# Masked sample products of a hybrid HGRN/RWKV decoder step, cut into 32-column and 32-row tiles of four sequences

## What is computed

```python
def trunk(x, ...):
    h = rmsnorm(x, norm_mix); proj = h @ w_in
    o_hg, s_hg = hgrn2_mix(q, f_pre, i_in, g_in, lb, st_hg, ...)   # 4 heads, 128x128 state
    o_rw, s_rw = rwkv7_mix(proj[..., HG_COLS:], p_prev, st_rw, ...) # 8 heads, 64x64 state
    x = x + concat([o_hg, o_rw]) @ w_out
    x = x + moe_ffn(rmsnorm(x), ...)      # top 4 of 32 experts, 1024 -> 2x1024 -> 1024
    return rmsnorm(x, norm_final), s_hg, s_rw, h[:, -1]

# per sample sequence b (the prompt starts from a zero state):
o_inter = einsum('bhtk,bhkv->bhtv', qc * exp(G), S)                       # HGRN read
S = exp(G_last) * S + einsum('bhsk,bhsv->bhkv', kc * exp(G_last - G), ic) # HGRN update
S = S * w + sa (x) (kk * a) + v (x) k                                     # RWKV update, per token
```

## Time and profile before

| | |
|---|---|
| median of three runs | 1248.78 us (1248.23 to 1252.48) |
| span of the profiled execution | 1244.8 us |
| that execution's own time | not recorded apart; the median is 4.0 us over the span |
| TensorE busy | 1211.9 us (97%) |
| VectorE busy | 460.2 us (37%) |
| ScalarE busy | 255.2 us (21%) |
| moved by DMA | 436.11 MB, mean 350 GB/s |
| chain that ended last | TensorE 77%, DMA 18%, VectorE 3%, ScalarE 1% |

### The profile page before, as it was taken

The page is one execution under the profiler, slowest core; times in us unless marked ns, Lnnn a source line. Parts: engine busy times, 40 slices in busy tenths (PEclk is TensorE's granted clock), DMA queues, the critical chain, the costliest instruction groups (busy, mean ns, idle before and its releaser), DMA issues.

```text
span 1244.8 us, 18279 instructions
## 1 busy us (share of the span) xinstructions
PE 1211.9 (97%) x7854; PEld 584.8 (47%) x7854; DVE 460.2 (37%) x958; ACT 255.2 (21%) x619; POOL 39.6 (3%) x94
## 2 busy tenths in 40 slices
PE   8999999999999999999999999999999999999997
PEld 5777776745443434444444434434443444343332
DVE  2356986754312331333233223313322233132224
ACT  2113432521311102111111111121111111111113
POOL 7000010000100000000000000000000000000000
PEclk9999999999999999999999999999999999999999
DMA  9732102484999999999999999999999999999994
GB/s 281 175 93 78 53 27 71 125 339 191 377 426 427 427 427 427 432 434 427 432 430 429 433 429 432 428 432 430 431 429 432 431 427 434 429 430 431 426 424 173
DMA packets 45244, 436.11 MB, mean 350 GB/s; under 512 B 9045, under 2 KB 24472, under 8 KB 29162
## 3 DMA queue, kind: packets, MB, share of 16 engines
q1 hardware_dynamic: 44036, 431.35, 83.8%
q0 software_dynamic: 1040, 3.54, 0.9%
q10 hardware_dynamic: 86, 0.02, 0.0%
HBM read 430.01 MB, written 4.89 MB: 349 GB/s over the span
## 4 chain that ended last, share of the span: by engine, by line
PE 77%; DMA 18%; DVE 3%; ACT 1%; issue 0%; SPq 0%; DVEq 0%; ACTq 0%
PE bank L1457 28%; PE bank L1491 14%; PE bank L812 10%; DMA ring<-in_w_gate_up 9%; PE bank L1432 7%; DMA mix<-in_w_gate_up 6%; PE bank L1521 4%; PE bank L1247 3%; DMA mix<-in_w_down 2%; PE bank L1482 2%; PE bank L1005 1%; PE bank L1512 1%; DVE mix L2316 1%; PE bank L839 1%; DMA hx<-in_state_shift 0%
## 5 line engine op out<-in xcount | busy, mean ns | idle before, releaser
L1457 PE MATMUL bank<-ring,mix 128*64 128x512 f32 x1568 | 355.5, 596 | 11.7 <-DMA ring<-in_w_gate_up 10.9
L1457 PEld LDWEIGHTS bank<-ring,mix 128*64 128x64 f32 x1568 | 108.7, 137 | 227.1 <-issue 216.6
L1491 PE MATMUL bank<-ring,mix 128*64 128x512 f32 x736 | 167.8, 598 | 0.0
L2674 DVE TENSOR_TENSOR hTb<-bank,w2a 128x512 f32<-128x512 f32 x32 | 22.1, 691 | 373.7 <-PE bank L1482 373.7
L812 PE MATMUL bank<-hTb,ring 128*128 128x320 f32 (+1 forms) x480 | 139.1, 443 | 1.3 <-issue 1.3
L1991 ACT ACTIVATE mix<-bank,nf 128x256 f32<-128x256 f32 x64 | 26.9, 471 | 458.9 <-PE bank L1432 458.9
L1457 PE MATMUL bank<-mix 128*64 128x512 f32 x480 | 112.1, 599 | 1.3 <-DMA mix<-in_w_gate_up 1.2
L812 PEld LDWEIGHTS bank<-hTb,ring 128*128 128x128 f32 x480 | 89.5, 191 | 39.6 <-issue 3.7
L2726 DVE TENSOR_TENSOR mix<-mix,bank 128x512 f32<-128x512 f32 x70 | 48.2, 689 | 161.3 <-PE bank L1521 161.3
L1491 PEld LDWEIGHTS bank<-ring,mix 128*64 128x64 f32 x736 | 49.7, 136 | 87.4 <-issue 83.3
L1432 PE MATMUL bank<-mix,hx 128*128 128x256 f32 x256 | 70.0, 416 | 0.0
(11 more groups left out here) (422 smaller groups left out, 1099.9 us busy)
## 6 DMA issues: line engine op xcount, KB each, us to landing
ring<-in_w_gate_up SPq DMA_DIRECT2D x34, 4096.0 KB, 27.1
ring<-in_w_down SPq DMA_DIRECT2D x17, 4096.0 KB, 28.8
ring<-in_w_gate_up SPq DMA_DIRECT2D x30, 2048.0 KB, 14.5
mix<-in_w_gate_up SPq DMA_DIRECT2D x12, 4096.0 KB, 25.8
mix<-in_w_down SPq DMA_DIRECT2D x6, 4096.0 KB, 29.0
ring<-in_w_down SPq DMA_DIRECT2D x11, 2048.0 KB, 16.5
ring<-in_w_in SPq DMA_DIRECT2D x15, 1024.0 KB, 6.2
mix<-in_w_gate_up SPq DMA_DIRECT2D x6, 2048.0 KB, 14.2
```

Source lines behind the costliest of these rows:

```text
L1457: last_ = mm(b_[64 * half:64 * half + 64, :].rearrange("s (p q) -> s p q", q=4), toks, cols[:, half], start=(c == 0), stop=(c == KT - 1))
L1491: last_ = mm(b_[r:r + 64, :], lhs, w[:, o:o + NCOL], start=(j == 0 and q == 0), stop=(j == 1 and q == 3))
L2674: v.tensor_tensor(halves(gg), halves(banks[3][:, :]), bias(e, 0), ALU.add).then_inc(S("g1"), 1)
```

## The change

It keeps the masks, but uses only those tokens of a mask that can be nonzero: four sequences are 32 tokens.

- `hosa`: sequence `q` is in half `part` of the sequences; the matmul takes only the 32 token columns of that half and writes only their 32 output partitions. There are still 32 matmuls (64 records), now 128 rows by 32 columns.
- `state_update`: the four sequences of half `part_` meet only their own 32 tokens, so a matmul has 32 rows. There are still 4 (8 records). All four banks are asked for ahead of the first matmul.
- `send`: the product is cut into the two halves of the sequences, 32 rows and 256 streamed columns each, so 8 matmuls (16 records) where 4 stood. The halves go to different banks: `sendl` (bank 2) takes sequences 0 to 3 of two `j_`, `sendh` (bank 5) sequences 4 to 7. A bank is filled and given back once per pair of `j_`.
- The order: `send(3)` follows `send(2)` directly, `own_values(1)` follows `own_values(0)`, and `centered(0)` comes behind it. On VectorE `sent(0)` moves behind the bonus.

```diff
-    add("send", 1, (2,))
     add("S0", 2, (3, 4))
-    add("send", 1, (5,))
+    add("sendl", 1, (2,))
+    add("sendh", 1, (5,))
     add("Q", 2, (0, 1))
-    add("send", 1, (2,))
-    add("Y0", 2, (6, 7), ended=False)
-    add("send", 1, (5,))
+    add("sendl", 1, (2,))
+    add("sendh", 1, (5,))
+    add("Y0", 2, (6, 7))
...
             for y in range(2):
-                for q in range(NS):
-                    for p in range(2):
-                        o = 576 * (2 * y + p) + 64 * q
-                        last = mm(b[64 * p:64 * p + 64, P * y:P * y + P], qm[:, o:o + 64], hs0[:, q, 2 * y + p, :],
-                                  start=(q == 0), stop=(q == NS - 1))
+                for q4 in range(NS // 2):
+                    for part in range(2):
+                        for p in range(2):
+                            q, r = 4 * part + q4, 64 * p + 32 * part
+                            o = 576 * (2 * y + p) + 64 * q + 32 * part
+                            last = mm(b[r:r + 32, P * y:P * y + P], qm[:, o:o + 32], hs0[:, q, 2 * y + p, :],
+                                      start=(q4 == 0), stop=(q4 == NS // 2 - 1))
...
                 pe.wait_ge(S("imask_ready"), jj + 1)
-                for half_ in range(2):
+                b_ = [free("hsend", 4 * jj + x_) for x_ in range(4)]
+                for part_ in range(2):
                     for p_ in range(2):
-                        b_ = free("hsend", 4 * jj + 2 * half_ + p_)
-                        filled(mm(b_[:, :], kstoks[half(p_), jj, :],
-                                  imask[half(p_), 4 * half_:4 * half_ + 4, :].rearrange("p b v -> p (b v)"),
+                        r_ = slice(64 * p_ + 32 * part_, 64 * p_ + 32 * part_ + 32)
+                        filled(mm(b_[2 * part_ + p_][:, :], kstoks[r_, jj, :],
+                                  imask[r_, 4 * part_:4 * part_ + 4, :].rearrange("p b v -> p (b v)"),
                                   start=True, stop=True), "hsend")
...
             def send(j_):
-                b_ = free("send", j_)
-                pe.wait_ge(S("Ys_ready"), 1)
-                pe.wait_ge(S("wr_ready"), 2)
-                for p_ in range(2):
-                    mm(b_[half(p_), :], bks[half(p_), 0, j_, :], um[j_][half(p_)].rearrange("p b v -> p (b v)"), start=True, stop=False,
-                       skip_group_check=True)
-                for p_ in range(2):
-                    last_ = mm(b_[half(p_), :], bks[half(p_), 1, j_, :], vm[j_][half(p_)].rearrange("p b v -> p (b v)"), start=False,
-                               stop=True, skip_group_check=True)
-                filled(last_, "send")
+                pair_, x_ = j_ // 2, 256 * (j_ % 2)
+                if x_ == 0:
+                    free("sendl", pair_)
+                    free("sendh", pair_)
+                    pe.wait_ge(S("Ys_ready"), 1)
+                    pe.wait_ge(S("wr_ready"), 2)
+                for term_, src_ in enumerate((um, vm)):
+                    for part_, stage_ in enumerate(("sendl", "sendh")):
+                        for p_ in range(2):
+                            r_ = slice(64 * p_ + 32 * part_, 64 * p_ + 32 * part_ + 32)
+                            last_ = mm(bank(stage_, pair_)[half(p_), x_:x_ + 256], bks[r_, term_, j_, :],
+                                       src_[j_][r_, 4 * part_:4 * part_ + 4].rearrange("p b v -> p (b v)"), start=(term_ == 0),
+                                       stop=(term_ == 1), skip_group_check=True)
+                        if term_ and x_:
+                            filled(last_, stage_)
...
             def sent(j):
-                b = wait_filled("send", j)[:, :].rearrange("p (q x) -> p q x", q=4)
-                for y in range(2):
+                for y, stage in enumerate(("sendl", "sendh")):
+                    b = wait_filled(stage, j // 2)[:, 256 * (j % 2):256 * (j % 2) + 256].rearrange("p (q x) -> p q x", q=2)
                     o = s0d[y][:, :, j].rearrange("p q c v -> p q (c v)")
-                    ins = v.tensor_tensor(o, o, b[:, 2 * y:2 * y + 2, :], ALU.add)
-                signal(ins, "send_ready")
+                    ins = v.tensor_tensor(o, o, b, ALU.add)
+                    if j % 2:
+                        signal(ins, f"{stage}_ready")
```

More of the change, by code:

```diff
@@ L196, in psum_units @@
     add("C", 2, (6, 7))
-    add("send", 1, (2,))
     add("S0", 2, (3, 4))
-    add("send", 1, (5,))
+    add("sendl", 1, (2,))
+    add("sendh", 1, (5,))
     add("Q", 2, (0, 1))
-    add("send", 1, (2,))
-    add("Y0", 2, (6, 7), ended=False)
-    add("send", 1, (5,))
+    add("sendl", 1, (2,))
+    add("sendh", 1, (5,))
+    add("Y0", 2, (6, 7))
     add("yc", 1, (2,))
-    end("Y0", 0)
-    end("Y0", 1)
     add("var", 1, (5,))
@@ L1360, in _ @@
             send(2)
+            send(3)
             bY_ = [free("Y0", 0), free("Y0", 1)]
@@ L1381, in _ @@
             own_values(0)
-            send(3)
-            centered(0)
             pe.wait_ge(S("y_part"), 2)
             own_values(1)
+            centered(0)
             chain(1)
@@ L1594, in _ @@
             gather_first(2)
-            for s, k in (("logit", 3), ("fold", 3), ("rank", 2), ("send", 4), ("yc", 3), ("var", 3)):
+            for s, k in (("logit", 3), ("fold", 3), ("rank", 2), ("sendl", 2), ("sendh", 2), ("yc", 3), ("var", 3)):
                 pe.wait_ge(S(f"{s}_ready"), k)
@@ L2606, in _ @@
             set_ci(0, 1)
-            sent(0)
             step_state(0)
@@ L2612, in _ @@
                                               op0=ALU.add, op1=ALU.mult), "bg_ready")
+            sent(0)
             sent(1)
```

## The result

The changed kernel takes 1251.63 us (median of 20 runs, 1249.49 to 1253.15), the kernel before 1249.26 us over 20 runs beside it. The ratio is 1.0022 with a 95% interval of 1.0014 to 1.003: about 2 to 4 us **slower** (0.2%, small but clear of the noise), where 2.0 us less were forecast and the range ended at 1250.3. Per profile row the edited products did what they should, and the loss came from a place in which the change puts no new wait.

What follows compares the result with a forecast made beforehand. VectorE was taken to bound the HGRN read, TensorE the RWKV updates, and TensorE and DMA the untouched expert part. Mixer savings less the new send(2) wait gave 2.0 us: 1248.78 to 1246.8 us, range 1244.3 to 1250.3.

Steps and rivals of the forecast that it cites:

- Expert part as one block: Last three quarters of the span: keeps its 929.9 us length, so what the mixer gains, the end gains.
- HGRN read, nothing on the path: At L935: TensorE 1.7 us shorter, but VectorE decides when L982 starts, so nothing is gained on the path.
- Four tiles at a time: In the three edited products: four 32-wide tiles run side by side, as the 64x64 tiles of L1355 do.
- The cost of switches in `send`: Around each send: a new pair of changes of tile shape, taken as 0.30 us.
- Both tile rivals: Edited products: 32-wide tiles run two at a time (1250.4 us, chance 0.08) or singly (about 1262, chance 0.04).
- HGRN updates, 1.08 less: From the HGRN updates to the C products: L1208 starts at 237.05 instead of 238.13.
- Wait at `send(2)`, 1.8 us: Before send(2): TensorE stands still 1.8 us for banks 2 and 5, given back after sent(1); start at 244.85.
- the sum: Mixer path through the HGRN updates, sends, wait and tail up to chain(1): 2.0 us less in all.
- the tail: From send(2) to chain(1): both own_values done by 248.9, chain(1) at 249.8 instead of 251.86.
- moves along: At L1107 in the first HGRN update's stretch: the 1.00 us pause without named releaser shifts with the code.
- the gain is eaten: Rival: copies between the places leave no slack, or L1107's pause recurs where own_values stand together; 1248.2 us, chance 0.17.
- The base: Whole kernel: the runs' median stands 4.0 us over the profiled span, 1248.78 us before the change.

Runs made afterwards that it cites:

- late loads: Changed kernel with the loads of w_out's second half and of x waiting for the units Y0: 1246.72 us, ratio 0.999 to the kernel before.
- only the x loads late: Changed kernel with only the three x loads waiting for Y0, w_out's second half loaded where it was: 1249.5 us, ratio 1.002 to the kernel before.
- real padding: Changed kernel with 16 of the Q matmuls done twice (64 instructions, same values): 1250.94 us, ratio 1.0026 to the kernel before.
- the HGRN part alone: Kernel before with only the change's HGRN read and two HGRN updates, RWKV update and orders as before: 1247.78 us against 1247.67, ratio 0.9999.

## Why the prediction was wrong

**Expert part as one block: right for this pair.** 929.7 against 929.9 us; over all profiles it lies between 929.4 and 931.3.

**HGRN read, nothing on the path: right.** L935 fell to 1.89 us, the wait for VectorE at L982 in its place:

```profile
153.14 1.16 PE L982 MATMUL bank<-mix 64*64 64x64 f32 x64 [1.81 <-DVE dc L2347]
```

It came at the first L982, which did not wait before, and the second kept its 0.7.

**Four tiles at a time: right.** 1.07 us for the first HGRN update (1.06 forecast), 1.31 for the second, 1.02 per `send` (1.16), 1.88 for the last two (2.05). The cost of switches in `send` was set 0.1 to 0.2 too high. Both tile rivals fell (the sum of the second gives 1262.7, not "about 1262", and that of the first, 1250.4, lies just outside the range that was said to take in most of it).

**HGRN updates, 1.08 less: too much.** From the first update to the first `send`, the three profiles without the new tiles take 30.8 to 31.2 us, the ten with them 30.05 to 31.25 with a median of 30.42: about 0.7 less. The changed kernel's own profile is the one with 31.25, in which no gain shows; its pause in L1108, the one of the earlier trace rows, is 1.46 us instead of 1.00. The second update takes 1.31 us and not 1.06, in four profiles with the new tiles alike, and waited 0.27 us for VectorE's L2394, not for ScalarE as worked out, and the `C` product for VectorE's copy by 0.55 as forecast.

**Wait at `send(2)`, 1.8 us: right in kind,** 1.55 measured. But it ends too late: from the first `send` to `send(2)` it takes 6.85 us where the sum has 5.9. The missing 1.0 lies ahead of VectorE's `step_state(0)`, which starts 3.15 us after the first `send` instead of 2.2, behind the pause of 0.68 us in `added_states(4, 8)`. The sum had no term for a new pause there.

**The step that failed** most is the tail: "`The two own_values take 0.9 each and 0.2 for the wait between them, to 248.9`". They took from 249.81 to 255.66, of which 3.25 us is the pause for the instruction block, and 1.5 more went at the lower clock behind it up to the output projection. No step of the sum asked whether TensorE's own instructions would be there in time; it put that at nothing. I had seen pauses of that kind, 1.00 us at L1107, and booked them as something that "moves along"; the rival "the gain is eaten" even named one where the `own_values` stand together, but at the price of the old one, 1.00 us. The price was the error: it was read in a stretch where the DMA share is 0.02, and used in one where the engines are full (1.00 from 252 to 254, above). That stretch of the kernel before:

```profile
208.90:225.80 16.90, 15.90 (x488) 12.34 (x480) 11.32 (x19) 5.92 (x21) 0.77 (x4) 1.00 0.02 4
```

The old pause is of the same kind: a transfer of the instruction queue starts at 215.56 and TensorE goes on at 218.05, 2.5 us later. With the long pause gone (late loads), the tail from `send(2)` to `chain(1)` takes 245.59 to 250.66, 5.1 us, against 4.95 forecast, and the kernel is 1 us faster than before, half of the forecast gain. The other half is the smaller gain of the HGRN updates and the pause in `added_states(4, 8)`, which is still there with 0.41 us.

**The base.** I put the profiled execution 4.0 us under its own median. In the later runs the time stands 2.1 over the span in each (1252.54 for a span of 1250.4). The profiled execution of before was thus one of the quick ones, about 1246.9, and the change in the two profiles, 5.6 us, is twice that of the medians; 0.9 of it lies ahead of `gM`, where the change does nothing that reaches TensorE's path.

## What to carry to other kernels

Packing small matmuls four to a turn also packs instructions: the same block of them passes in less time, so ask when the next block of code is fetched and what the DMA engines do then. An idle of TensorE with no releaser in dense code, next to a large load, is a candidate for that, and moving the load, not the code, is the cheap remedy; price it by a row with the same DMA load. A pause of 3 us can cost once more behind itself by the clock, here 1.5 us.

## What the runs showed of the hardware

- A transfer of 16 KB of instructions started 1.1 us after the block ahead began with idle DMA engines and 4.0 us after with 3.3 MB of loads queued; TensorE went on 2.3 us after it started in the first and 2.7 us in the second.
- The place of the pause is a count: record 3496 in five kernels with different orders and padding.
- 32-row tiles of 64 columns that share output partitions but write different banks ran four together, 16 records of 256 columns in 1.02 us.
- TensorE's granted clock fell to 0.50 after an idle of 3.25 us at 255 and stayed at 1.00 after one of 2.15 us (only the x loads late) and one of 2.34 us (real padding). The idle time alone does not decide it: in the run of the HGRN part alone it stayed at 1.00 after an idle of 3.25 us that ended at 1140.9.
